# Streams' attention on one core: each pair of heads on a quarter of the array's columns, in place of zero-padded full-width products

## What is computed

```python
def fox_block(qi, cq, qpos, k, v, ck):      # per stream: 16 queries, 1024 + 16 keys, 8 heads of 64
    scale = FOX_DIM ** -0.5
    logits = jnp.einsum('bqhd,bkhd->bhqk', qi, k, preferred_element_type=jnp.float32) * scale
    logits = logits + cq[..., :, None] - ck[..., None, :]
    mask = jnp.arange(k.shape[1])[None, :] <= qpos[:, None]
    logits = jnp.where(mask, logits, -jnp.inf)
    p = jax.nn.softmax(logits, axis=-1).astype(v.dtype)
    return jnp.einsum('bhqk,bkhd->bqhd', p, v)
```

## Time and profile before

| what | us |
|---|---|
| three runs | 3852.27, 3853.20, 3856.85 |
| median | 3853.2 |
| profiled execution: span, first to last instruction | 3845.6 |
| TensorE busy in it | 3706.3 (96%) |
| VectorE, ScalarE, GpSimd busy | 1626.1 (42%), 1171.5 (30%), 337.2 (9%) |
| mean granted clock of TensorE | 0.989 |

### The profile page before, as it was taken

How to read it: one execution, slowest core, us unless ns; L and a number is a source line. 1 busy time by engine, 2 the same in 40 slices (tenths; PEclk the granted TensorE clock), 3 DMA queues, 4 the chain that set the end, 5 groups by cost and what they waited for, 6 DMA issues and landing times. The chain is left out here.

```text
span 3845.6 us, 53670 instructions
## 1 busy us (share of the span) xinstructions
PE 3706.3 (96%) x20456; PEld 3204.3 (83%) x20456; DVE 1626.1 (42%) x3504; ACT 1171.5 (30%) x2318; POOL 337.2 (9%) x416
## 2 busy tenths in 40 slices
PE   8999999899999999998998999999999999999998
PEld 8999999777777677776667889999999999888886
DVE  4000377655545454544434444444444444432222
ACT  5122222334333333332213333333333333321111
POOL 3000000212111111211200000000000000000000
PEclk9999999899999999999999999999999999999999
DMA  4212322410222212124333331111111111442222
GB/s 156 70 63 65 87 69 70 87 41 24 61 46 46 53 26 48 32 87 144 134 139 105 117 95 46 46 45 45 45 45 45 45 45 48 138 135 82 80 82 67
DMA packets 328015, 278.83 MB, mean 73 GB/s; under 512 B 97106, under 2 KB 292802, under 8 KB 326781
## 3 DMA queue, kind: packets, MB, share of 16 engines
q1 hardware_dynamic: 318207, 258.03, 22.6%
q0 software_dynamic: 5216, 18.23, 1.4%
q10 hardware_dynamic: 4416, 0.14, 0.1%
HBM read 190.70 MB, written 85.65 MB: 72 GB/s over the span
## 5 line engine op out<-in xcount | busy, mean ns | idle before, releaser
L2617 PE MATMUL bank<-ffn_hn_hi,ffn_w_parts 128*128 128x436 f32 (+1 forms) x3520 | 986.4, 361 | 2.2 <-ACTq L2724 2.2
L2617 PEld LDWEIGHTS bank<-ffn_hn_hi,ffn_w_parts 128*128 128x128 f32 x3520 | 661.2, 188 | 38.9 <-issue 2.6
L2617 PE MATMUL bank<-ffn_hn_lo,ffn_w_parts 128*128 128x436 f32 (+1 forms) x1760 | 634.1, 360 | 0.0
L416 PE MATMUL bank<-in_xh,in_wh 128*128 128x436 f32 (+1 forms) x1280 | 357.6, 360 | 2.9 <-DVE in_wh L634 2.9
L2617 PEld LDWEIGHTS bank<-ffn_hn_lo,ffn_w_parts 128*128 128x128 f32 x1760 | 330.8, 188 | 19.3
L2651 PE MATMUL bank<-ffn_down_wa,ffn_g_hi 128*128 (+1 forms) x1224 | 328.9, 391 | 3.9 <-DVE ffn_g_lo L2946 3.9
L2753 ACT COPY ffn_raw<-bank 128x436 f32<-128x436 f32 (+1 forms) x220 | 110.5, 502 | 703.9 <-PE bank L2617 649.4
L1552 PE MATMUL bank<-heads_p_pT,heads_p_v 128*65 128x512 f32 (+3 forms) x640 | 286.4, 529 | 10.3 <-issue 9.8
L2880 DVE TENSOR_SCALAR ffn_hist<-ffn_raw 128x2 f32 (+2 forms) x264 | 45.0, 170 | 546.8 <-ACT ffn_acc L2757 544.0
L2651 PEld LDWEIGHTS bank<-ffn_down_wa,ffn_g_hi 128*128 128x128 f32 x1224 | 230.0, 188 | 53.4 <-DVE ffn_down_wa L2943 3.3
L416 PEld LDWEIGHTS bank<-in_xh,in_wh 128*128 128x128 f32 x1280 | 241.3, 189 | 14.7 <-DVE in_wh L634 3.3
(11 more groups left out here) (418 smaller groups left out, 6369.5 us busy)
## 6 DMA issues: line engine op xcount, KB each, us to landing
ffn_w<-in_w_up_dram SPq DMA_DIRECT2D x44, 512.0 KB, 5.0
ffn_g_raw<-scratch_g SPq DMA_DIRECT2D x110, 192.0 KB, 2.3
scratch_g<-ffn_acc SPq DMA_DIRECT2D x88, 218.0 KB, 2.0
heads_s_k<-in_cache_fox_k_dram SPq DMA_DIRECT2D x8, 2048.0 KB, 13.6
heads_s_v<-in_cache_fox_v_dram SPq DMA_DIRECT2D x8, 2048.0 KB, 8.3
heads_d_qkvT<-scratch_gch SPq DMA_DIRECT2D x17, 768.0 KB, 5.6
ffn_y<-in_w_down_dram SPq DMA_DIRECT2D x22, 512.0 KB, 3.7
scratch_gch<-in_work SPq DMA_DIRECT2D x48, 218.0 KB, 1.9
```

Source lines behind the costliest of these rows:

```text
L416: mm = pe.matmul(bank[:, 4 + i % 2, 0:wide], a[:, k, :], b[:, k, col:col + wide], start=(k == 0 and m == 0), stop=(k == KD - 1 and m == 2))
L2617: mm = pe.matmul(bank[:, pair(n) + e, 0:width], w_parts[a][:, part, e, k, :], x[:, k, cols], start=(k == 0 and m == 0), stop=(k == KD - 1 ...
```

## The change

The operands of the four products of a logits bank are cut to the 32 columns of weights of their pair, and write the 32 output rows of that pair only. The products of new keys with queries likewise; the 40-row product now comes first and the four pairs add to it. The values of a pair of heads are multiplied by the probabilities of that pair only: 32 columns of weights, 128 columns of values, output 32 rows x 128 columns; so one product of 512 columns becomes four of 128. `out` then works on 128 columns instead of 512, with a mask of 2 columns (`half_of`, made once), and its reduction sums 2 numbers instead of 8. A bank of logits is issued whole, at the due time of its former second half.

```diff
-        self.all_heads = self.q_tok[:].rearrange("p (h d) -> p h d", d=FD)
+        self.both_heads = self.q_tok[:, 0:P].rearrange("p (e d) -> p e d", d=FD)
...
-        def logits_of(b, g, half):
+        def logits_of(b, g):
             a, out, keys = b % 2, self.bank[:, self.logit[g], :], slice(g * BANK, (g + 1) * BANK)
...
+            pe.matmul(out, self.pick[:, a, :], self.sums[:, keys], start=True, stop=False)
+            for p in range(NP):
+                pair = slice(p * PAIR, (p + 1) * PAIR)
+                mm = pe.matmul(out[pair], self.q_heads[:, a, p, pair], self.kT[:, p, keys], start=False, stop=True)
+            mm.then_inc(s["s_mm"], 1)
...
             for p in range(NP):
-                pe.matmul(out, self.q_heads[:, a, p, :], self.kT_new[:, p, cols], start=(p == 0), stop=False)
-            if b == 0:
-                pe.wait_ge(s["new_ready"], 10)
-            pe.matmul(out, self.new_l[:], self.new_r[:, cols], start=False, stop=True).then_inc(s["s_mm"], 1)
+                pair = slice(p * PAIR, (p + 1) * PAIR)
+                mm = pe.matmul(out[pair], self.q_heads[:, a, p, pair], self.kT_new[:, p, cols], start=False, stop=True)
+            mm.then_inc(s["s_mm"], 1)
...
         def values(b, part):
-            a, out = b % 2, self.bank[:, self.last, :]
+            a, out = b % 2, self.bank[:, self.last, 0:P]
+            pairs = [(slice(p * PAIR, (p + 1) * PAIR), slice(p * P, (p + 1) * P)) for p in range(NP)]
...
-                pe.matmul(out, self.pT_new[:], self.v_new[:, a, :], start=True, stop=False)
+                for rows, cols in pairs:
+                    pe.matmul(out[rows], self.pT_new[:, rows], self.v_new[:, a, cols], start=True, stop=False)
...
-                mm = pe.matmul(out, self.pT[:, n, :], self.v[:, a, n, :], start=False, stop=n == NK - 1)
+                for rows, cols in pairs:
+                    mm = pe.matmul(out[rows], self.pT[:, n, rows], self.v[:, a, n, cols], start=False, stop=n == NK - 1)
...
-                for n in range(4):
-                    yield at + 3.0 * n
-                    if b == 0 and n == 0:
-                        pe.wait_ge(s["new_ready"], 8)
-                    logits_of(b, n // 2, n % 2)
+                for g in range(2):
+                    yield at + 3.0 + 6.0 * g
+                    if b == 0 and g == 0:
+                        pe.wait_ge(s["new_ready"], 9)
+                    logits_of(b, g)
...
-            nc.vector.scalar_tensor_tensor(self.all_heads, self.bank[:, self.last, :].rearrange("p (h d) -> p h d", d=FD),
+            nc.vector.scalar_tensor_tensor(self.both_heads, self.bank[:, self.last, 0:P].rearrange("p (e d) -> p e d", d=FD),
                                            self.inv_sum[:, b % 2:b % 2 + 1],
-                                           spread(c["stream_rows"][:].unsqueeze(2), [P, FH, FD]), ALU.mult, ALU.mult) \
+                                           spread(self.half_of[:].unsqueeze(2), [P, 2, FD]), ALU.mult, ALU.mult) \
                 .then_inc(s["o_out"], 1)
```

More of the change, by code:

```diff
@@ L1717, in __init__ @@
         self.head_of, self.stream_of = ph.sb("s_head_of", [P, FH]), ph.sb("s_stream_of", [P, DB])
+        self.half_of = ph.sb("s_half_of", [P, 2])
         self.s = {n: ph.sem("s_" + n) for n in (
@@ L1812, in tensor @@
         s, c, NP, NK, DB, DS = self.s, self.c, self.NP, self.NK, self.c["DB"], self.c["DS"]
-        ident = c["ident"][:]
+        ident, PAIR = c["ident"][:], 2 * DS
         def suffix_sums():
@@ L1831, in turn_k @@
             mm.then_inc(s["kt_mm"], 1)
-        def logits_of(b, g, half):
+        def logits_of(b, g):
             a, out, keys = b % 2, self.bank[:, self.logit[g], :], slice(g * BANK, (g + 1) * BANK)
[L1835 to L1845, removed]
+            if g == 0:
+                pe.wait_ge(s["q_ready"], 3 * b + 3)
+            after(pe, s["pt_out_v"], 2 * b) if g == 0 else after(pe, s["pt_out_a"], b)
+            pe.wait_ge(s["kt_out_v"], (NK // 2) * b + 2 * g + 2)
+            pe.wait_ge(s["kt_out_a"], (NK // 2) * b + 2 * g + 2)
+            pe.matmul(out, self.pick[:, a, :], self.sums[:, keys], start=True, stop=False)
[3 more added lines that the diff above has]
+            mm.then_inc(s["s_mm"], 1)
         def logits_new(b):
             a, cols, out = b % 2, slice(b * DS, (b + 1) * DS), self.turned_bank(0)[:, 0:DS]
+            if b == 0:
+                pe.wait_ge(s["new_ready"], 11)
+            pe.matmul(out, self.new_l[:], self.new_r[:, cols], start=True, stop=False)
             for p in range(NP):
-                pe.matmul(out, self.q_heads[:, a, p, :], self.kT_new[:, p, cols], start=(p == 0), stop=False)
-            if b == 0:
-                pe.wait_ge(s["new_ready"], 10)
-            pe.matmul(out, self.new_l[:], self.new_r[:, cols], start=False, stop=True).then_inc(s["s_mm"], 1)
+                pair = slice(p * PAIR, (p + 1) * PAIR)
+                mm = pe.matmul(out[pair], self.q_heads[:, a, p, pair], self.kT_new[:, p, cols], start=False, stop=True)
+            mm.then_inc(s["s_mm"], 1)
         def turn_p(b):
@@ L1891, in tensor @@
         yield self.begin + 7.8
-        pe.wait_ge(s["new_ready"], 5)
+        pe.wait_ge(s["new_ready"], 6)
         pe.matmul(self.bank[0:32 + c["FH"], self.last, 0:P], self.f_new[:], c["tri_s"][:], start=True, stop=True) \
@@ L1995, in out @@
             dve.wait_ge(s["pv_mm"], b + 1)
-            nc.vector.scalar_tensor_tensor(self.all_heads, self.bank[:, self.last, :].rearrange("p (h d) -> p h d", d=FD),
+            nc.vector.scalar_tensor_tensor(self.both_heads, self.bank[:, self.last, 0:P].rearrange("p (e d) -> p e d", d=FD),
                                            self.inv_sum[:, b % 2:b % 2 + 1],
-                                           spread(c["stream_rows"][:].unsqueeze(2), [P, FH, FD]), ALU.mult, ALU.mult) \
+                                           spread(self.half_of[:].unsqueeze(2), [P, 2, FD]), ALU.mult, ALU.mult) \
                 .then_inc(s["o_out"], 1)
             dve.wait_ge(s["o_out"], b + 1)
-            nc.vector.tensor_reduce(self.o[:, b, :], self.all_heads.rearrange("p h d -> p d h"), AX.X, ALU.add) \
+            nc.vector.tensor_reduce(self.o[:, b, :], self.both_heads.rearrange("p e d -> p d e"), AX.X, ALU.add) \
                 .then_inc(s["o_ready"], 1)
@@ L2007, in vector @@
         nc.vector.tensor_reduce(self.stream_of[:], ident[:].rearrange("p (e b h) -> p b e h", e=2, b=DB), AX.XY, ALU.add) \
+            .then_inc(s["new_ready"], 1)
+        nc.vector.tensor_reduce(self.half_of[:], c["stream_rows"][:].rearrange("p (m e) -> p e m", e=2), AX.X, ALU.add) \
             .then_inc(s["new_ready"], 1)
@@ L2028, in vector @@
         nc.vector.memset(self.new_l[:], 0.0).then_inc(s["new_ready"], 1)
-        dve.wait_ge(s["new_ready"], 5)
+        dve.wait_ge(s["new_ready"], 6)
         cp(self.new_l[0:DS].rearrange("q (h r) -> q h r", r=DS),
@@ L2039, in vector @@
         cp(self.kT_new[:], self.bank[:, self.logit[1], :].rearrange("p (c t) -> p c t", t=P)).then_inc(s["new_ready"], 1)
-        dve.wait_ge(s["new_ready"], 8)
+        dve.wait_ge(s["new_ready"], 9)
         parts(0)
```

## The result

The changed kernel takes **3784.3 us** (four runs, 3778.4 to 3787.9) where the kernel before takes 3855.0 (3852.3 to 3857.3): ratio 0.9815, interval 0.980 to 0.983, 71 us or 1.8% less. I had predicted 3822, with 3810 as the lower end, and had given the case in which all four quarters work side by side (rival 3, 3774 us) a chance of 3%. That case is what happened.

The account below looks back on a forecast made before the run. TensorE, busy 289 of 313 us of the streams' attention, sets that stage's length. Sum: -18.7 - 5.1 - 1.6 - 15.7 + 10.1 - 7 + 7.4 = -30.6 us, so 3853 - 31 = 3822 us; range 3810 to 3864.

Parts of the forecast that it names:

- rival 3: All four quarters work side by side, second records not holding back the next pair: about -79 us, 3774 us; chance 0.03.
- (a): Logits of past keys: partial overlap cuts a bank from 3.44 to 2.27 us, saving 18.7 us.
- rival 1: No overlap: quarters take turns, each held until the other's columns are through; +7.2 us, 3860 us; chance 0.14.
- (c): Values, new keys: two records of 0.43 us become four products taking 0.67 us, saving 1.6 us.
- (d): Values, past keys: a block falls from 0.86 to 0.56 us, saving 15.7 us.
- (b): Logits, new keys: shorter weight loads, 0.25 instead of 0.89 us a stream, save 5.1 us.
- (e): TensorE's changes between full and partial array: 102 instead of 30, at 0.12 or 0.20 us each, cost 10.1 us.
- (f): VectorE's `out` on 128 instead of 512 columns: 0.72 us together, shortening waits and the end; saves 7 us.
- (g): Lost cover between Delta's steps, as logits go out in whole banks: eight waits of 0.93 us cost 7.4 us.
- rival 4: Overlap comes, but turned-key copies and Delta's chain take back about half, or the clock falls: 3838 us; chance 0.09.

Follow-up runs that it names:

- Experiments 1 and 2: 1: values' products ordered quarter by quarter inside a part, in the changed kernel: 3785.1 us; 2: its past-key logits on two 64-column halves, not four quarters: 3794.0 us.
- Experiment 4: The changed kernel with the logits of a bank issued again in two halves, at the due times of before: 3786.7 us.

## Why the prediction was wrong

- **(a) is the step that failed.** It said: "The two records of one product sit on the same quarter and follow each other. If the next pair starts 0.03 us after the second record has started". The first half is right: they start 0.43 apart. The second is wrong: the second record waits in its own quarter and holds back nobody else, so the next pair starts 0.007 us after the *first* record. A bank takes 0.43 + 0.43 + 0.1 and not 2.27 + 0.1. Experiments 1 and 2 bear this mechanism out: a part of the values takes the same 0.6 us in either order, and two parts at work in place of four cost 12.7 us, of 13.6 expected. I had carried the rule that each record follows the one before over from a trace in which all records use the whole array, though rival 1 named that very objection.
- **(c) and (d)** failed by the same step. A block of values takes 0.22 to 0.25 us, and not 0.56; rival 3 had 0.31 because it still charged 0.03 per product, where 0.007 is enough.
- **(b)** was right, -5.7 against -5.1.
- **(e)** was right in the 0.09 us of a change and wrong in the loads added to it. At the higher clock level L1841, the full product ahead of each bank (of type fp32r, one record), is 0.41 us from the next start, where it was 0.31 (its sum is 7.5 us, 5.9 before, part of that at the lower level). Out of a bank it is 0.54 from the start of the second four, 0.43 and 0.1 more. So a change costs 0.1 both ways, where I had 0.12 and 0.20; 72 more changes make about 7 us by this estimate, not 10.1. All of it lies inside the sums above.
- **(f)** 7 us predicted. The two steps take 0.35 + 0.29 = 0.64 us, of 0.72 expected. That is worth 3.4 us of waits for turned keys, 1.1 at the end, and 0.3 each ahead of the turning of p and of the new values: about 5.
- **(g)** 7.4 predicted; 8.6 by the distances, 11 by the waits for Delta's results. Eight waits of 0.93 became more waits, of 0.78 us. Experiment 4 took 8 of it back.
- **Missing: the end of the stage** (+6.9). "Whatever shortens the stage shortens the kernel by as much" holds down to the next thing that was nearly as late. That was the store of the states.
- **Missing: the clock**, named in rival 4 but in none of my terms. L960 and L957 took 6.0 us more. That is not all net: up to the last product the lower level was granted for 27.3 us before and for 34.1 after. Of this 7.3 and 19.6 us fell on L960 and L957. Before, the rest made other lines longer. And only one execution of before was profiled, a quick one, so a part of the 6.0 may be its luck.

Rival 3 had the mechanism right. Its sum was added up wrongly: 39.8 + 5.1 + 4.4 + 35.2 - 10.1 + 7 - 7.4 is 74, not 79, so its time is 3779 and not 3774. The measured 3784 is 5 us above that; the end of the stage and the clock are more than enough for it, and (a) to (d) came to 88.0 us where it had 84.5. Its chance of 3% rested on one sentence ("today each follows the one before it"), and no row bore on it either way. A mechanism that no row excludes, worth 40 us more than the one preferred, should have had more, and the low end of the range should have reached it.

## What to carry over

Products that need only part of the array's columns are worth placing on separate parts: four of 32 columns took little more than the time of one, and so did two of 64 columns, and a quarter's products may stand one behind the other; a whole group then costs as little as a half, so don't split it to fill gaps. Ahead of a large cut in one engine's work, list what ends within the size of that cut before the stage's end (here a store of 2 MB, 13 us ahead), and see whether it can go out in parts or earlier. Putting the waits for it last, alone, gave no gain that could be told from noise; with the store in two it was 6 us, at the edge of the noise.

## What I had not expected of the hardware

The granted clock. In the changed kernel TensorE ran at the lower of its two levels (1.2 GHz) for 27.3 us from 1900.7 on; before, two stretches of 6.8 us fell in the same work, at 1948.9 and 1965.9. Each of these times TensorE was at Delta's products of 16 columns (L960, with L957 between them) when it fell. Shorter stretches of 3.4 us began elsewhere in the stage, before and after. One group of 16 such records at the higher and one at the lower level, and the logits bank at the lower:

```profile
1897.16 1.86 PE L960 MATMUL bank<-heads_d_qn,heads_d_S_s 128*128 128x16 f32 x16
...
1901.64 3.43 PE L960 MATMUL bank<-heads_d_qn,heads_d_S_s 128*128 128x16 f32 x16
...
1925.47 1.94 PE L1844 MATMUL bank<-heads_p_tok,heads_s_q_heads 128*32 128x512 f32 x8
```

In the profiles of all twelve runs above, 27 to 38 us of the lower level fell in that work, in one or two pieces, even where logits or values were full width. I made no run that moves this work elsewhere, so what the change has to do with it stays open.
